# Window attention by query tile: four heads side by side, value products in three products of rounded parts

## What is computed

```python
def window_attention(q, k, v, q_norm_g, k_norm_g, sink):   # 8 query heads of 128, 2 key/value heads
    q = apply_rope(rms_norm(q...)); k = apply_rope(rms_norm(k...))
    def one_block(args):                                    # one block of 128 queries
        ki, vi = three blocks of 128 keys and values around the query block
        s = jnp.einsum('bqgrd,bkgd->bgrqk', qi, ki) * scale
        s = jnp.where(valid, s, NEG)                        # band of +-128, inside the sequence
        p = jax.nn.softmax(jnp.concatenate([s, sink_l], axis=-1), axis=-1)[..., :-1]
        o = jnp.einsum('bgrqk,bkgd->bqgrd', p, vi)
```

## Time and profile before

| | us |
|---|---|
| median of 3 runs | 2104.8 (2104.61 to 2106.28) |
| the profiled execution: its own time | 2103.86 |
| the profiled execution: its span | 2102.0 |
| stretches of gate and attention, group 0, 1, 2 | 88.6, 92.4, 92.3 |

### The profile page before, as it was taken

One profiled execution on the slowest core, in us unless ns is written; L12 is line 12 of the kernel. 1 busy time (PEld: TensorE's weight loads), 2 busy tenths in 40 slices (PEclk: granted clock), 3 DMA queues, 4 the chain that ended last, 5 costly groups with the idle time before them and its releaser, 6 DMA issues.

```text
span 2102.0 us, 30582 instructions
## 1 busy us (share of the span) xinstructions
PE 2077.5 (99%) x10396; PEld 1747.5 (83%) x10396; DVE 1298.5 (62%) x1688; ACT 1075.0 (51%) x1584; POOL 465.2 (22%) x656
## 2 busy tenths in 40 slices
PE   9999999999999999999999999999999999999998
PEld 8898888888888888898988888757888888888886
DVE  5764233465654233466653434369999999998995
ACT  5553332344542332345533232238888888887884
POOL 4252011210451011213510102002222222112321
PEclk9999999999999999999999999999999999999999
DMA  8213323443123322452123225497998689999892
GB/s 237 90 42 112 91 80 100 141 170 101 61 57 118 100 81 81 175 172 75 41 89 92 80 81 178 181 356 260 372 385 310 235 318 334 383 381 372 287 347 65
DMA packets 108739, 380.00 MB, mean 181 GB/s; under 512 B 13522, under 2 KB 19843, under 8 KB 83044
## 3 DMA queue, kind: packets, MB, share of 16 engines
q1 hardware_dynamic: 91812, 335.64, 44.3%
q0 software_dynamic: 16832, 43.08, 7.6%
HBM read 403.31 MB, written 34.60 MB: 208 GB/s over the span
## 4 chain that ended last, share of the span: by engine, by line
PE 48%; DMA 4%; DVE 2%; issue 2%; ACT 1%; POOL 0%; POOLq 0%; SPq 0%; DVEq 0%; ACTq 0%
PE main L551 3%; PE main L552 3%; PE main L553 3%; DMA held_wu<-w_up_e 3%; PE main L2063 3%; PE main L2065 3%; PE main L2064 3%; PE main L2051 3%; PE main L2050 3%; PE main L2049 3%; PE aux L2049 3%; PE aux L2051 3%; PE aux L2050 3%; PE main L539 2%; PE main L541 2%; PE main L540 2%
## 5 line engine op out<-in xcount | busy, mean ns | idle before, releaser
L1009 DVE TENSOR_TENSOR w_lo<-raw,w_hi 128x1024 fp32r<-128x1024 f32 (+1 forms) x216 | 251.3, 1183 | 273.9 <-ACT w_hi L753 273.7
L753 ACT ACTIVATE w_hi<-raw 128x1024 fp32r<-128x1024 f32 (+1 forms) x216 | 211.8, 1006 | 141.7 <-PE main L553 72.7
L551 PE MATMUL main<-e_g_hi,w_hi 128*128 128x512 f32 x576 | 235.7, 409 | 0.0
L553 PE MATMUL main<-e_g_hi,w_lo 128*128 128x512 f32 x576 | 225.6, 392 | 0.0
L552 PE MATMUL main<-e_g_lo,w_hi 128*128 128x512 f32 x576 | 225.2, 391 | 0.0
L2209 DVE TENSOR_TENSOR e_d_lo<-held_wd,e_d_hi 128x2048 fp32r<-128x2048 f32 x76 | 174.0, 2291 | 51.4 <-ACT e_d_hi L2135 51.2
L539 PE MATMUL main<-w_hi,e_g_hi 128*128 128x512 f32 (+1 forms) x560 | 203.2, 363 | 0.6 <-DVE e_g_lo L1023 0.6
L541 PE MATMUL main<-w_hi,e_g_lo 128*128 128x512 f32 (+1 forms) x560 | 200.0, 357 | 0.0
L540 PE MATMUL main<-w_lo,e_g_hi 128*128 128x512 f32 (+1 forms) x560 | 199.8, 357 | 0.0
L2209 DVE TENSOR_TENSOR e_u_lo<-held_wu,e_u_hi 128x2048 fp32r<-128x2048 f32 x76 | 173.7, 2287 | 13.7 <-ACT e_u_hi L2135 13.7
L2209 DVE TENSOR_TENSOR e_g_lo<-held_wg,e_g_hi 128x2048 fp32r<-128x2048 f32 x76 | 173.7, 2286 | 4.4 <-ACT e_g_hi L2135 4.3
(11 more groups left out here) (378 smaller groups left out, 4716.2 us busy)
## 6 DMA issues: line engine op xcount, KB each, us to landing
held_wg<-w_gate_e SPq DMA_DIRECT2D x78, 1024.0 KB
held_wu<-w_up_e SPq DMA_DIRECT2D x78, 1024.0 KB
held_wd<-w_down_e SPq DMA_DIRECT2D x76, 1024.0 KB
raw<-w_in SPq DMA_DIRECT2D x120, 512.0 KB, 3.8
raw<-w_proj_b SPq DMA_DIRECT2D x24, 512.0 KB, 3.7
raw<-w_proj_a SPq DMA_DIRECT2D x24, 512.0 KB, 3.8
raw<-w_out SPq DMA_DIRECT2D x24, 512.0 KB, 4.3
raw<-w_in SPq DMA_DIRECT2D x24, 256.0 KB, 4.4
```

The source lines that it names most:

```text
L551: pe.matmul(bank[:], hi[:, k, :], mov_hi[:, k, :], start=(k == 0), stop=False)
L553: mm = pe.matmul(bank[:], lo[:, k, :], mov_hi[:, k, :], start=False, stop=(k == KT - 1))
L753: act.activation(hi, buf, ACT.Copy).then_inc(w_hi_done, 1)
L1009: dve.tensor_tensor(lo, buf, hi.bitcast(F32), ALU.subtract).then_inc(w_split, 1)
```

## The change

A unit is now one query tile of one key/value head and one of its four query heads: `unit(s)` gives `i = s // 4` (8 query tiles of the two key/value heads), `n = i % 4` and `r = s % 4`, so four slots in a row share their keys, values and mask. The four heads' transposed weights stand side by side in one tile `pT`, and `values(g, i)` makes the four heads' value product at once, with 512 columns, from rounded parts. For this ACT rounds the transposed weights of each unit (`pT_hi`) and DVE makes the rest (`pT_lo`), both in the slot after the transposes, one ahead of the `Exp` and one ahead of the mask of that slot; the values are split into `va_hi` and `va_lo` once per group. `Exp` now works in place in `pr`, and `sm` and `pt` are gone. There is one `pT_hi` and one `pT_lo`, for one query tile. `oT` and `qT` are laid out by query tile, and the panels `PPB` read `oT` through a strided view.

```diff
+def unit(s):
+    return s // REP, s // REP % GT, s % REP
...
-    pt = [place(f"pt{i}", [P, 3 * P], F32, Dd + 1536 * i) for i in (0, 1, 4)]
-    sm = [place("sm0", [P, 3 * P], F32, Dd + 3072), place("sm1", [P, 3 * P], F32, Dd + 9216)]
+    pT_hi, pT_lo = (place(name, [P, 3, REP, P], F32R, Dd + 3072 + 6144 * i) for i, name in enumerate(("pT_hi", "pT_lo")))
...  tensor(pe), attend(g, s)
+            if s % REP == 0 and s >= 2 * REP:
+                values(g, s // REP - 2)
...
-            if 0 <= s - 5 < NU:
-                ...
-                for i, c in enumerate(ch):
-                    v = va[:, n + c, (h // REP) * HD:(h // REP + 1) * HD]
-                    mm = pe.matmul(bank[:, n * P:(n + 1) * P], v, pt[u % 3][:, i * P:(i + 1) * P], start=(i == 0), stop=(c == ch[-1]))
-                mm.then_inc(o_ps, 1)
+        def values(g, i):
+            kv, n = divmod(i, GT)
+            ch = chunks(g, n)
+            pe.wait_ge(pt_ready, NU * g + REP * (i + 1))
+            pe.wait_ge(va_lo_done, VA_SPLIT[g])
+            bank = take_bank(o_bank[i % 2], (o_done, NQT * g + i + 1))
+            for x, c in enumerate(ch):
+                ...
+                pe.matmul(bank[:], v_hi, p_hi, start=(x == 0), stop=False)
+                pe.matmul(bank[:], v_hi, p_lo, start=False, stop=False)
+                mm = pe.matmul(bank[:], v_lo, p_hi, start=False, stop=(c == ch[-1]))
+            mm.then_inc(o_ps, 1)
...  scalar(act), attend(g, s)
+            if 0 <= s - 4 < NU:
+                u = s - 4
+                i, n, r = unit(u)
+                act.wait_ge(pt_ps, NU * g + u + 1)
+                if r == 0 and i:
+                    act.wait_ge(o_ps, NQT * g + i)
+                act.activation(pT_hi[:, 0:w, r, :], pt_bank[u % 2]..., ACT.Copy).then_inc(pt_hi_done, 1)
             if s < NU:
                 act.wait_ge(negm_ready, NU * g + s + 1)
-                if s >= 4:
-                    act.wait_ge(pt_ps, NU * g + s - 3)
-                act.activation(pr[s % 4][:, 0:w], sm[s % 2][:, 0:w], ACT.Exp, ...)
+                act.activation(pr[s % 4][:, 0:w], pr[s % 4][:, 0:w], ACT.Exp, ...)
...
+            if s == 1:
+                act.wait_ge(q_roped, 8 * g + 8)
+                for x in range(1 + (g > 0)):
+                    act.activation(va_hi[x], va[:, va_slots(g, x), :], ACT.Copy).then_inc(va_hi_done, 1)
+            if s % REP == 0 and s >= 2 * REP:
+                i = s // REP - 2
+                act.wait_ge(o_ps, NQT * g + i + 1)
+                act.activation(oT_hi[:, i, :], o_bank[i % 2][:], ACT.Copy).then_inc(o_hi_done, 1)
...  vector(dve), attend(g, s)
+            if 0 <= s - 4 < NU:
+                u = s - 4
+                dve.wait_ge(pt_hi_done, NU * g + u + 1)
+                dve.tensor_tensor(pT_lo[:, 0:w, r, :], pt_bank[u % 2]..., pT_hi[...], ALU.subtract).then_inc(pt_ready, 1)
             if s < NU:
                 dve.wait_ge(s_ps, NU * g + s + 1)
-                if s >= 2:
-                    dve.wait_ge(exp_done, NU * g + s - 1)
+                if s >= 4:
+                    dve.wait_ge(pt_ps, NU * g + s - 3)
                 dve.tensor_tensor_reduce(...)
                 dve.tensor_scalar(st[:, 1:2], ...).then_inc(negm_ready, 1)
-            if 0 <= s - 3 < NU:
-                u = s - 3
-                dve.wait_ge(pt_ps, NU * g + u + 1)
-                dve.tensor_copy(pt[u % 3][:, 0:w], pt_bank[u % 2][:, 0:w]).then_inc(pt_ready, 1)
+            if s == 2:
+                for x in range(1 + (g > 0)):
+                    dve.tensor_tensor(va_lo[...], v, va_hi[x].bitcast(F32), ALU.subtract).then_inc(va_lo_done, 1)
```

More of the change, by code:

```diff
@@ L59 @@
 NU = NH * GT
+NQT = NKV * GT
 PADS = 2 * G
@@ L97, with va_slots @@
 OUT = {key: n + 1 for n, key in enumerate((g, p, j) for g in range(NG) for p, j in work_of(g))}
+VA_SPLIT = [1, 3, 5]
+def va_slots(g, x):
+    first = (g < 2) + GT * x
+    return slice(first, first + (1 if x else GT))
+def unit(s):
+    return s // REP, s // REP % GT, s % REP
 def kv_at(g, t):
@@ L546, in feature_major, with tokens @@
             slots = list(slots)
+            out = bank[:]
+            if p in (PPB, PPB + 1):
+                out = out.rearrange("p (n q) -> p n q", n=GT)
+            def tokens(t, k):
+                return of_head(t, k) if p in (PPB, PPB + 1) else t[:, k, :]
             hi, lo = w_hi[p % 2][:, :, j * P:(j + 1) * P], w_lo[p % 2][:, :, j * P:(j + 1) * P]
@@ L841, in attend @@
                 act.wait_ge(negm_ready, NU * g + s + 1)
-                if s >= 4:
-                    act.wait_ge(pt_ps, NU * g + s - 3)
-                act.activation(pr[s % 4][:, 0:w], sm[s % 2][:, 0:w], ACT.Exp, bias=stat[:, s % 8, 1:2],
+                act.activation(pr[s % 4][:, 0:w], pr[s % 4][:, 0:w], ACT.Exp, bias=stat[:, s % 8, 1:2],
                                scale=rsq[:, s:s + 1], accum_out=stat[:, s % 8, 2:3])
@@ L866, in copy_qT @@
             q, t = i // GT, i % GT
[L867 to L868 removed]
+            act.activation(qT_hi[:, GT * q + t, :], q_bank(i)[:], ACT.Copy).then_inc(turned_hi, 1)
         def copy_va(g, t, bank):
@@ L1303, in attend @@
-            for u in ((s - 6, s - 5) if s == NU + 4 else (s - 6,)):
-                h, n = divmod(u, GT)
-                if 0 <= u < NU and n == GT - 1:
-                    dve.wait_ge(o_hi_done, NH * g + h + 1)
-                    dve.tensor_tensor(oT_lo[:, h, :], o_bank[h % 2][:], oT_hi[:, h, :].bitcast(F32),
-                                      ALU.subtract).then_inc(o_done, 1)
+            if s == 2:
+                for x in range(1 + (g > 0)):
+                    dve.wait_ge(va_hi_done, VA_SPLIT[g] - (g > 0) + x)
+                    v = va[:, va_slots(g, x), :]
+                    dve.tensor_tensor(va_lo[:, va_slots(g, x), :], v, va_hi[x].bitcast(F32), ALU.subtract).then_inc(va_lo_done, 1)
@@ L1310, in mixed @@
+            for i in [s // REP - 2] * (s % REP == 1 and s > 2 * REP) + [NQT - 1] * (s == NU + 4):
+                dve.wait_ge(o_hi_done, NQT * g + i + 1)
+                dve.tensor_tensor(oT_lo[:, i, :], o_bank[i % 2][:], oT_hi[:, i, :].bitcast(F32),
+                                  ALU.subtract).then_inc(o_done, 1)
         def mixed(g, c):
@@ L1315, in mixed @@
                 if g == 0:
-                    dve.wait_ge(misc_in, 2 * 16)
+                    dve.wait_ge(misc_in, 3 * 16)
+            if g == 1 and c == 0:
+                dve.wait_ge(halo_kept, 1)
             if c >= 2:
@@ L1524, in gpsimd @@
         pool.memset(minus, -1.0)
-        pool.memset(half, -0.5).then_inc(const_set, 1)
-        pool.wait_ge(const_set, 1)
+        then(pool.memset(half, -0.5))
         norm_x(0, 0)
```

134 lines of the change are left out of this document (68 added, 66 removed).

## The result

The changed kernel takes 2161.86 us (median of 6 runs, 2157.18 to 2165.54), the kernel before 2104.7 (6 runs beside them): ratio 1.0266, 95% interval 1.0251 to 1.0282. The forecast was 2160, with 2136 to 2176 as its range. The profiled execution took 2160.73 us, its span is 2158.7.

The account below looks back on a forecast made before the run. PE was taken to bound the kernel before. The ring costs +49.6 us, the part ahead of it +9, the part behind -3: +55.6 on 2103.9 gives 2159.5, so 2160 us for the median, range 2136 to 2176.

Parts of the forecast that it names:

- The ring: ACT and DVE, mask(4) to mask(31): Exp, rounding, rest and mask follow in turn, 2.78 us a round; costs +49.6 us.
- bare turns: Between mask(4) and mask(31): 81 turns of 2.78 us, less 5.3 and 4.8 for two-block turns: 215.1 us.
- Insertions: On ACT between Exp and next rounding: weight roundings, Tanh, oT_hi, qT_hi add in full, 12.6 a group, 37.8 us.
- Waits for the value product inside the ring: A query tile's first rounding waits for the value product before: .6 us at two places a group, 4 in all.
- Ahead of the ring: Group start up to mask(4): splitting the values makes mask(3) 1.3 us late; +3.0 a group, +9 in all.
- Behind it: After mask(31) to the next panel: only PE has sizable work, 10.0 to 11.0 us; -1 a group, -3 in all.
- PE's gain: Value products on PE: 256 float32 products (56.9 us) out, 192 rounded (43.6) in; 13.3 us if PE sets the pace.
- PE's pace holds: Rival: in the stretches the ring overlaps somewhere, PE sets the pace, 13.3 us are gained: 2091.5 us; chance .07.
- The clock: Rival: PE's short waits in the stretches bring the 1.2 GHz clock, some +240 us, 2345; chance .02.
- The range: 2136 (roundings .39, -7; half the insertions hidden, -19) to 2176 (roundings .58, +8; DVE's extras uncovered, +8); chance .78.
- PE's share: Profile sign: PE busy for 77 to 81% of the gate and attention stretches, which last 106 to 112 us.
- The rule weighed: ACT, DVE and GpSimd are strictly first in, first out: 2160 us by the rule, 2091.5 without it.

Follow-up runs that it names:

- e1: The changed kernel with DVE's rest (pT_lo) moved behind mask and bias of the same slot; 2108.7 us, 1.0012 of the kernel before.
- e7: The changed kernel with DVE making both pT_hi and pT_lo, ahead of its mask, and ACT no part of it; 2105.0 us, .9991 of the kernel before.
- e8: The changed kernel with two one-column copies to a spare tile ahead of each rounding on ACT; 2181.0 us, 1.0348 of the kernel before.
- e3: The changed kernel with two of the three value products left out, only hi x hi kept; 2150.6 us, 1.0207 of the kernel before.
- e2: The changed kernel with oT_hi, qT_hi, Tanh and weight roundings held back behind the next slot's pT_hi on ACT; 2123.1 us, 1.0076 of the kernel before.
- e5: e1 with the value product behind the slot's scores and transposes on PE; 2106.5 us, .9999 of the kernel before.
- e6: e5 with the held-back ACT insertions of e2; 2106.8 us, .9999 of the kernel before.
- e9: e5 with the values split tile by tile over slots 3 to 6 and the last queries turned two steps earlier; 2104.2 us, .9984 of the kernel before.
- e4: The changed kernel's regrouping in plain float32, without rounding or split, DVE copying ahead of its mask; 2106.0 us, .9990 of the kernel before.
- e11: e9 with a slot's transposes and value product one gate step later on PE; 2105.9 us, .9999 of the kernel before.
- e12: e7 with value product behind, values split tile by tile, last queries turned earlier, transposes one gate step later; 2120.2 us, 1.0068 of the kernel before.

## Why the prediction was right

**The ring.** From mask(4) to mask(31) the groups took 83.9, 88.0 and 88.1 us, 259.9 in all against 207.3: +52.6, forecast +49.6. The round of 2.78 measured 2.77; turns with two blocks 2.53 or 2.29, where the deductions made 2.54 to 2.56 (one half of the turn) and 2.32 (both). The roundings took .47 and .37 us for 384 and 256 columns, forecast .48 and .39; insertions .48 and .95. e1 and e7 remove the ring and with it the loss, e8 lengthens it and 74 of 81 turns follow, e3 shows that PE isn't it. By terms the 259.9 us are 213.8 for the bare turns (forecast 215.1), 37.1 for the insertions (37.8) and 9.0 for the rest (4); so the good agreement is one of the terms and not only of the sum, but for the last.

**Insertions.** 37.8 forecast, 37.1 by the steps in the trace. e2 gives back 34.3 us between mask(4) and mask(31), because other waits grow by 2.8, which its expectation had as 3.

**Waits for the value product inside the ring.** 4 us forecast, 9.0 measured: the one term that was clearly mis-sized. Eight turns are longer than their links and insertions make them, each behind ACT's wait for a value product. Where nothing is inserted and the clock did not fall they are .8 to 1.0 us longer, where the sum had .6; the two with a fall are 1.94 and 2.25 longer.

**Ahead of the ring.** +9 forecast, +7.5 measured (from the first scores product to mask(4): 10.9, 11.4 and 12.6 us, before 9.0, 9.0 and 9.4).

**Behind it.** -3 forecast, -3.5 measured (9.9, 10.9, 9.9 against 11.1, 11.6, 11.4). The total is nearer than its parts: the ring came out 3.0 us over its forecast, the other two 2.0 under theirs, and that these cancel is luck.

**PE's gain.** 13.3 us if PE sets the pace, 4.4 a group. It didn't, and the sum took it as hidden; the price itself was somewhat high: 3.0 us per group by the steps, with some waits still in them, and a rounded product steps by .24 and not .227. What was wrong was the rival built on it. "PE's pace holds" was priced at 2091.5, but e1, e5 and e6, where the ring is gone, end at 2107 to 2109. PE's pace with the new order isn't the old pace less the gain, because transposes come late for their bank (8.0 us in e5, 9.9 in e9), which they never did before.

**The clock.** The rival said +240 or nothing. A small part of it came: 2.3 us of the 52.6, below. The prediction read the clock before as the upper level in every slice; a 9 in that view means 90% or more, and the trace has a fall of 3.4 us at 1197.8, outside the stretches, and one at its end.

**The range.** Its two ends were priced loosely. With .39 for all roundings the 59 turns with three key blocks give 5 us and not 7, and with .58 all 81 give 10 and not 8. The measured time lies inside the range either way.

**PE's share.** 77 to 81% forecast for the stretches, 83% measured. A likely reason: a product's record lasts .39 us where its step is .23, so the end of the last one ahead of each wait counts as busy; and some ran at the lower clock.

**The rule weighed.** The rows agree with it: in the changed kernel the rounding starts right behind each insertion and the turn grows by the whole step, and in e2 the same instructions, one place further back, lie in ACT's wait.

## What to carry to other kernels

Before moving work between two engines, write down the order on each and look for a path that leaves one engine, crosses to the other and comes back within one slot. Its length counts, not the busy shares: 52% and 60% busy engines held a 96% busy TensorE up by 57 us, and one instruction put behind its neighbour undid it. Insert side work behind the link of the ring, not ahead of it. When the ring is open, look next at a buffer that is freed once in several slots: whatever stands behind its waiter on an in-order engine can be late, and a later order on TensorE makes it later. And before a wait is explained, check the named releaser against the code: where an instruction waits for two things, a view may name an engine that had merely ended last.

## What the runs showed of the hardware

**The clock fell behind short gaps in the middle of busy stretches.** In the profiled execution of the changed kernel the granted clock fell to 1.2 GHz for 3.4 us at 598.0 and at 1058.8 us; in those of the kernel before and of e1, e2, e4 to e7 and e9 to e11 it never fell inside a stretch. PE's timeline around the first (a wait of .48, then of 1.36 for the turned queries, then steps of .43 where the earlier trace rows have .23):

```profile
595.93 0.52 PE L626 MATMUL main<-ident,pr 128*128 128x128 f32 x3 [0.48 <-DVE pT_lo L1323]
597.82 0.66 PE L574 MATMUL main<-e_g_hi,w_hi 128*128 128x512 f32 x1 [1.36 <-DVE qT_lo L1313]
598.27 0.63 PE L575 MATMUL main<-e_g_lo,w_hi 128*128 128x512 f32 x1
598.70 0.63 PE L576 MATMUL main<-e_g_hi,w_lo 128*128 128x512 f32 x1
...
601.96 0.39 PE L575 MATMUL main<-e_g_lo,w_hi 128*128 128x512 f32 x1
```

and the windows of it (columns as in the earlier trace rows):

```profile
596.00:599.00 3.00, 1.64 (x6) 1.21 (x7) 2.73 (x8) 1.36 (x4) 1.15 (x3) 0.83 0.30 113
599.00:602.00 3.00, 3.00 (x12) 2.50 (x12) 1.05 (x5) 1.84 (x5) 1.51 (x4) 0.60 0.00 0
602.00:605.00 3.00, 3.00 (x15) 2.45 (x14) 0.55 (x3) 0.99 (x3) 1.13 (x3) 1.00 0.00 0
```

The masks of these slots were 4.71 and 4.54 us apart, where turns of the same columns with the same wait and no fall have 3.58 and 3.33: 2.3 us for both. It came with more waiting: none in e2, two in the changed kernel, four in e3, five in e8 (and one in e12); in e8 it adds to the .18 per turn. The Trainium skill, "TensorE: Matmul & The Clock Gate", HAM oscillation, says that idle gaps bring the slow clock back, and its example has waits of several microseconds; here no single gap ahead of the falls in the changed kernel was over 1.4 us. Which gaps do it is open: in the same kernel PE waits 1.72 us at 641.0 and in e7 1.18 us at 573.5 with no fall.

**Small ScalarE instructions overlap.** Two copies of one column start .19 us ahead of the next instruction, together (e8), though one lasts .19 by itself.
